# A decoder layer of gMLP, sparse attention and MLP on one core: two early tiles in a place of their own, a state copy cut into eight, norm sums moved, the last tile in halves

## The chip, the core and the metric

The kernel runs on one core of one Trainium2 chip. The metric is the device time of one execution in microseconds (us); lower is better. The median of three runs is 2820.18 us (2817.41 to 2821.86).

## What is computed

One layer for 512 prompt rows and 8 sample rows (TOK = 520 columns in the kernel, kept transposed, features on partitions), all in float32:

```
h   = rmsnorm(x) ; z = h @ w_in              # kv pairs, queries, v and u of the gMLP, gates
A   = u * (tril(w_sgu) @ rmsnorm(v) + b_sgu) # per chunk of 128 rows and per channel group
B   = gates * (compressed, selected, window attention)  # 8 heads, T5 bias; samples use caches and state
mix = sigmoid(g_a) * (A @ w_proj_gmlp) + sigmoid(g_b) * (B @ w_proj_nsa)
x2  = x + mix @ w_out
y   = x2 + square(relu(rmsnorm(x2) @ w_up)) @ w_down
```

Also returned: the raw k and v rows, the last chunk of v, and for the 8 samples the window state (`win`), which is a plain copy of the input `state` (8 x 256 x 512 floats, 4.2 MB) with one row appended on the host.

## The kernel before, in words

Five engine programs are written out by hand and synchronised by semaphores; each engine runs its list in order, so what stands where in each list is the schedule. Every product is done in three passes on rounded parts: a weight tile `w` is split into `w_hi` (ScalarE, ACT) and `w_lo` = w - w_hi (VectorE, DVE), the moving operand into `a_hi` and `a_lo`, and TensorE (PE) adds hi*hi, lo*hi and hi*lo. SP loads the raw weights.

**Units.** The products ahead of the MLP are 68 units plus 16 and 16 (`unit`, line 508): one unit is 128 output rows, 16 row tiles of x in 4 chunks c = 0 to 3 of 24 matmuls. ACT and DVE run `beside(u, jobs)`: for each chunk they split one chunk of the next unit, and then do `jobs[c]`, so a job at index c comes behind the split of chunk c. PE does `hooks[c]` behind chunk c: small products for the attention. Order: 12 kv units, 8 query units, 16 units of v and u (pairs, one pair for each sample b: the sample's attention is hooked into it, `smp_pair`), 32 gate units (four for each head h, with the prompt's attention), 16 projection units, 16 output units that give x2.

**Places of the change.**
- The first kv units go to the two tiles `z[:, 0]` and `z[:, 1]`, are scaled there (`first_scale`, 1325), stored from there by an ACT queue (`store`, 1007) and copied by GpSimd (POOL, 1939). `z_free` (1329) makes DVE wait for store and copy before unit n+2 overwrites the tile. Behind it in DVE's list stand `rel_rows` and the splits; PE waits for `rel_done` (616).
- Sample pair 0: at index 1 DVE does `windows_turned` (1419), which PE's hook 2 (`smp_values(0)`, `smp_turn_keys(0)`) waits for.
- After the last sample pair PE does `norm_sum(N_NORM_V)` into PSUM banks 4 and 5 (`aux[:, 0:2]`), waits until DVE's `mean` has read it, and starts the scores of head 0.
- POOL issues the copy `win <- state` as one DMA (2015) when v is normed, in head 0. The gate tiles' stores `merge_d <- z` (2023) are issued behind it, and DVE waits for them (`g_stored`, 1648).
- Between the gate units and the projections, the 16 mixed tiles are split to `a_hi`, `a_lo` (`mixed_chunk`): tiles 0 to 3 in the last gate unit, 4 to 15 behind it. The loads `g_in` (2034) wait for the last gate store.
- The MLP runs in NG = 16 groups. A group has 2 x 7 block products (`product`; r = 0, 1 and b = 0 to 6, block i = 7r + b; a Strassen-like scheme with weight sums `w_sums`) and 16 down tiles (`down_part`). Weights stay in 4 raw slots; `HI_RING` names the place of each block's `w_hi`. Eight-fold operand tiles `at_t` are made from x2; the last (index 7, from x2 tiles 14 and 15) can only be made when the last output unit is done: `first_pair` (1812). The sum of squares of x2 is gathered by POOL (`x2_spill`), summed over partitions by `norm_sum(N_NORM_X2)` in `up_first` (897), and turned into 1/rms by `x2_base`, `x2_guess`, `x2_scale`.
- At the end, for each of 16 output tiles: `y_in` adds the last down sum, `y_out` multiplies by r squared and adds x2, SP stores (502).

Of the kernel before, what the change touches and what calls it, by code (L numbers as in the profile page):

```python
# [42 lines left out]
EPS = 1e-6  # L43
# [35 lines left out]
HI_RING = (0, 1, 2) * 6 + (1, 0, 1, 2)  # L79
# [53 lines left out]
def build(nc, t):  # L133
    with ExitStack() as ctx:
# [75 lines left out]
        x_two = at("x_two", [P, KT, TOK], zone)  # L210
        u_t = at("u_t", [P, GRP, TOK], r1)
# [112 lines left out]
        norm_base = sem("norm_base")  # L324
        norm_guess = sem("norm_guess")
# [43 lines left out]

        aux3_made, aux3_read = sem("aux3_made"), sem("aux3_read")  # L370
# [12 lines left out]
        ff_used, ff_out = sem("ff_used"), sem("ff_out")  # L383
# [75 lines left out]
        def _(sp_):  # L459
# [47 lines left out]
        def _(pe):  # L507
# [34 lines left out]
            def norm_sum(n, src=None, made=None):  # L542
# [5 lines left out]
                for h in range(2):  # L548
                    last = pe.matmul(aux[:, h, 0:HT], ones[:, :], src[:, h * HT:(h + 1) * HT],  # L549
# [219 lines left out]
            with pe.Fori(1, DEC) as b:  # L769
# [119 lines left out]
            def up_first():  # L889
# [13 lines left out]
            def down_part(g, u, kts):  # L903
                o = DOWN_BANKS[u % 4]
                i = 2 * NP + u // 2
                for kt in kts:
# [3 lines left out]
                    for w, a, part in ((wh, fb_hi, 0), (wh, fb_lo, 1), (wl, fb_hi, 2)):  # L910
                        for h in range(2):
# [1252 lines left out]
```

## Time and profile before

| what | value |
|---|---|
| median of 3 runs | 2820.18 us |
| the profiled execution | 2819.64 us, its span 2818.0 us |
| mean granted TensorE clock | 0.994 |
| PE busy | 2792.2 us (99%) |
| weight loads | 2747.7 us (98%) |
| DVE, ACT, POOL busy | 56%, 34%, 8% |
| DMA engines, mean over the span | 110 GB/s |
| chain that ended last | PE 95%, DVE 2%, DMA 1%, ACT 1%, issue 1% |

Busy time is a share of the span; PE's is matmuls as the profile models them, so it can be busy and not at full rate. The clock is 1.00 at 2.4 GHz and 0.50 at 1.2 GHz; a stretch's value is the mean over it.

### The profile page before, as it was taken

The page shows a single profiled execution, that of the slowest core. Times are in us where ns is not written, and L with a number is a line of the kernel's source. Part 1 is how long each engine was busy: PE and PEld are TensorE (multiplying, and loading weights), DVE is VectorE, ACT ScalarE, POOL GpSimd, SP SyncE. Part 2 cuts the span into 40 slices and gives each one's busy share as a digit, 9 for nine tenths or more (in the row PEclk, how much of TensorE's full clock was granted, in tenths as well). Part 3 has the DMA queues.
Part 4 walks back from the last instruction along what each step waited for, and adds up shares of the span by engine and source line. Part 5 has one row for each costly group of instructions (what it writes and reads, how often), then busy time and mean ns, then how long its engine had stood idle before and what let it go on. Part 6 is the DMA issues. An engine that isn't in the chain of part 4 may idle for free.

```text
span 2818.0 us, 57713 instructions
## 1 busy us (share of the span) xinstructions
PE 2792.2 (99%) x22723; PEld 2747.7 (98%) x22723; DVE 1576.8 (56%) x2759; ACT 958.9 (34%) x1481; POOL 224.0 (8%) x337
## 2 busy tenths in 40 slices
PE   8999999999999999999999999999999999999999
PEld 8999899999999999999999999999999999999999
DVE  5433554454444454445576566665566655666658
ACT  5435433333333342223243223332233322333322
POOL 2100122210000010013310000000000000000000
PEclk9999999999999999999999999999999999999999
DMA  6533233342222224444432323322232223332225
GB/s 199 187 101 106 75 112 97 108 147 96 87 93 95 90 87 149 135 127 136 140 103 87 101 90 104 104 90 88 89 116 97 95 79 106 102 104 97 89 97 184
DMA packets 89235, 309.27 MB, mean 110 GB/s; under 512 B 11586, under 2 KB 11714, under 8 KB 89104
## 3 DMA queue, kind: packets, MB, share of 16 engines
q1 hardware_dynamic: 70112, 247.63, 27.0%
q0 software_dynamic: 16032, 55.42, 6.0%
q10 hardware_dynamic: 3024, 5.32, 0.6%
q8 instruction: 45, 0.74, 0.1%
q14 instruction: 22, 0.18, 0.0%
HBM read 287.23 MB, written 27.37 MB: 112 GB/s over the span
## 4 chain that ended last, share of the span: by engine, by line
PE 95%; DVE 2%; DMA 1%; ACT 1%; issue 1%; POOL 0%; SPq 0%; DVEq 0%; ACTq 0%; POOLq 0%
PE mm L535 39%; PE mm L912 13%; PE aux L912 13%; PE mm L857 12%; PE aux L857 9%; PE aux L640 1%; PE mm L609 1%; PE aux L794 1%; DMA merge_d<-z 1%; PE aux L783 1%; PE aux L784 1%; PE aux L807 1%; PE aux L805 1%; PE aux L549 0%; PE aux L756 0%
## 5 line engine op out<-in xcount | busy, mean ns | idle before, releaser
L1259 DVE TENSOR_TENSOR w_lo<-w_raw,w_hi 128x512 fp32r<-128x512 f32 x392 | 280.2, 716 | 632.7 <-ACT w_hi L954 631.5
L1738 DVE TENSOR_TENSOR w_lo<-w_raw,w_hi 128x1024 fp32r<-128x1024 f32 x288 | 352.8, 1225 | 390.1 <-ACT w_hi L1184 149.3
L535 PE MATMUL mm<-a_hi,w_hi 128*128 128x260 f32 x2624 | 549.0, 291 | 3.2 <-DVE rel_s L1293 2.0
L535 PE MATMUL mm<-a_hi,w_lo 128*128 128x260 f32 x2624 | 531.9, 284 | 0.0
L535 PE MATMUL mm<-a_lo,w_hi 128*128 128x260 f32 x2624 | 531.4, 284 | 0.0
L1184 ACT ACTIVATE w_hi<-w_raw 128x1024 fp32r<-128x1024 f32 x288 | 297.6, 1056 | 656.9 <-PE mm L912 432.6
L954 ACT ACTIVATE w_hi<-w_raw 128x512 fp32r<-128x512 f32 x392 | 246.3, 629 | 691.7 <-PE mm L535 668.5
L535 PEld LDWEIGHTS mm<-a_hi,w_hi 128*128 128x128 f32 x2624 | 408.4, 190 | 10.0 <-DVE w_lo L1259 3.5
L535 PEld LDWEIGHTS mm<-a_lo,w_hi 128*128 128x128 f32 x2624 | 408.6, 190 | 0.0
L535 PEld LDWEIGHTS mm<-a_hi,w_lo 128*128 128x128 f32 x2624 | 408.1, 190 | 0.0
L857 PE MATMUL mm<-at_t,w_hi 128*128 128x260 f32 x2048 | 372.8, 284 | 4.2 <-DVE at_t L1830 3.3
L857 PEld LDWEIGHTS mm<-at_t,w_hi 128*128 128x128 f32 x2048 | 316.4, 189 | 6.7 <-issue 3.5
L857 PE MATMUL mm<-at_t,w_lo 128*128 128x260 f32 x1024 | 289.5, 283 | 0.0
L857 PE MATMUL aux<-at_t,w_hi 128*128 128x260 f32 x1536 | 278.3, 283 | 1.0 <-DVE w_lo L1738 1.0
L857 PEld LDWEIGHTS aux<-at_t,w_hi 128*128 128x128 f32 x1536 | 236.7, 188 | 1.6 <-DVE w_lo L1738 1.6
L857 PE MATMUL aux<-at_t,w_lo 128*128 128x260 f32 x768 | 217.0, 283 | 0.0
L912 PE MATMUL aux<-fb_lo,w_hi 128*128 128x260 f32 x1024 | 207.6, 284 | 0.0
L912 PE MATMUL mm<-fb_lo,w_hi 128*128 128x260 f32 x1024 | 207.4, 284 | 0.0
L912 PE MATMUL mm<-fb_hi,w_lo 128*128 128x260 f32 x1024 | 206.2, 283 | 0.0
L912 PE MATMUL aux<-fb_hi,w_lo 128*128 128x260 f32 x1024 | 205.8, 282 | 0.0
L912 PE MATMUL mm<-fb_hi,w_hi 128*128 128x260 f32 x1024 | 205.4, 282 | 0.0
L912 PE MATMUL aux<-fb_hi,w_hi 128*128 128x260 f32 x1024 | 205.3, 282 | 0.0
(312 smaller groups left out, 4164.4 us busy)
## 6 DMA issues: line engine op xcount, KB each, us to landing
w_raw<-in_w_ff SPq DMA_DIRECT2D x256, 512.0 KB, 3.6
w_raw<-in_w SPq DMA_DIRECT2D x200, 512.0 KB, 3.7
merge_d<-z POOLq DMA_DIRECT2D x32, 260.0 KB, 2.4
g_in<-merge_d POOLq DMA_DIRECT2D x16, 520.0 KB, 4.8
x_back<-x_d POOLq DMA_DIRECT2D x8, 520.0 KB, 9.1
out_y_t<-y_acc SPq DMA_DIRECT2D x16, 260.0 KB, 2.0
pages<-in_cache_cmp POOLq DMA_DIRECT2D x16, 256.0 KB, 3.4
w_cmp<-in_w_cmp POOLq DMA_DIRECT2D x8, 512.0 KB, 4.6
```

The costliest lines, as they stand in the source:

```text
L535: last = pe.matmul(mm[:, 2 * v + h, 0:HT], w, a[:, kt, h * HT:(h + 1) * HT], start=first and k == 0 and part == 0, stop=final and k == CK ...
L609: last = pe.matmul(mm[:, 2 * u + h, 0:HT], w, a[:, kt, h * HT:(h + 1) * HT], start=kt == 0 and part == 0, stop=kt == KT - 1 and part == 2)
L640: last = pe.matmul(aux[:, 2 + kv, 0:NKV * (W_ALL + 1)], w_cmp[:, n % 2, jj, :], kv_t[:, NKV * kv:NKV * (kv + 1), j % STRIDE, j // STRIDE:j ...
L783: pe.matmul(aux[:, 0, 0:P * (i + 1)], qi, k_t[:, g, 0:P * (i + 1)], start=True, stop=True)
L784: pe.matmul(aux[:, 1, 0:P * (i + 1)], qi, k_t[:, 2 + g, 0:P * (i + 1)], start=True, stop=True)
L794: pe.transpose(aux[:, n, k * P:(k + 1) * P], src[:, k * P:(k + 1) * P], ident[:, :])
L857: last = pe.matmul(bank(BANKS[r][b]), w, at_t[:, j, e:e + HT], start=FRESH[b] and j == 0 and part == 0, stop=j == KP - 1 and part == 2, sk ...
L912: last = pe.matmul(bank(o + h), w, a[:, kt, h * HT:(h + 1) * HT], start=kt == 0 and part == 0, stop=kt == 3 and part == 2)
L954: run(w_hi[:, c, :], raw(u, c), ACT.Copy).then_inc(hi_split, 1)
L1184: run(ring_hi(i), fold(source(i)), ACT.Copy).then_inc(ff_hi, 1)
L1259: dve.tensor_tensor(w_lo[:, c, :], raw(u, c), w_hi[:, c, :].bitcast(F32), ALU.subtract).then_inc(lo_split, 1)
L1738: dve.tensor_tensor(ring_lo(i), fold(source(i)), ring_hi(i).bitcast(F32), ALU.subtract).then_inc(ff_lo, 1)
```

## The change

Eight edits at once:

1. `z_first` = two tiles of `x_two` hold units 0 and 1; `z_free` waits only from unit 4 on.
2. Sample pair 0: the hook and the jobs of index 2 go to index 3.
3. The sum for v's norm goes to banks 6 and 7 and ahead of the last sample's `attend`; waits for the banks move into `scores`.
4. The state copy leaves head 0; it becomes 8 DMAs, one for each sample, sample b when group b of the MLP has ended.
5. Mixed tiles 4 to 7 are split at index 3 of the last gate unit instead of behind it.
6. The start of the MLP: ACT makes one of the two scaled operands, `HI_RING` swaps places 1 and 2 so that block 1 does not wait for a weight sum, the operands come in three portions, and PE does block 1's product over index 6 late.
7. x2's norm: the last square by ACT in a tile of its own, the sum over partitions ahead of block 3, the guess and its Newton step spread over group 0 (tiles 12 to 15 of `y_acc`).
8. Last tile: `y_acc` is scaled and added early, the last down sums come half by half, two 133 KB stores, the second from ACT's queue. For this the last group stands outside PE's loop.

```diff
-HI_RING = (0, 1, 2) * 6 + (1, 0, 1, 2)
+HI_RING = (0, 2, 1) * 6 + (2, 0, 2, 1)
...
+        z_first = x_two[:, 2 * CH:2 * CH + 2, :]
...
+            sp_.wait_ge(y_done, MB)
+            sp_.dma_start(t["y_t"][MB - 1][:, 0:HT], y_acc[:, MB - 1, 0:HT]).then_inc(y_stored, 16)
...
-            smp_pair(0, [lambda: norm_sum(n_norm_q(NH - 1)), turn_windows,
+            smp_pair(0, [lambda: norm_sum(n_norm_q(NH - 1)), turn_windows, None,
                          lambda: (smp_values(0)(), smp_turn_keys(0)())])
-            pe.wait_ge(smp_read, DEC)
-            norm_sum(N_NORM_V, acc_v, (v_acc, GRP))
-            pe.wait_ge(norm_base, N_NORM_V + 1)
+            smp_pair(DEC - 1, [smp_values(DEC - 1), None, smp_turn_keys(DEC - 1)],
+                     lambda: norm_sum(N_NORM_V, acc_v, (v_acc, GRP), 2))
...
+                    pe.wait_ge(smp_read, DEC)
                     pe.matmul(aux[:, 1, 0:P * (i + 1)], qi, k_t[:, 2 + g, 0:P * (i + 1)], start=True, stop=True)
+                    pe.wait_ge(norm_base, N_NORM_V + 1)
...
+                    if b in (2, 3) and r == 0 and type(g) is int and g == 0:
+                        pe.wait_ge(at_ready, KP + b - 1)
+                    if b == 3 and r == 0 and type(g) is int and g == 0:
+                        norm_sum(N_NORM_X2, y_acc[:, MB - 4, :], (x2_added, 1))
...
-                product(0, 1, range(KP - 1))
-                norm_sum(N_NORM_X2, acc_x, (x2_squared, MB))
+                product(0, 1, range(KP - 2))
                 pe.wait_ge(at_ready, KP)
                 product(0, 0, [KP - 1])
-                product(0, 1, [KP - 1])
+                product(0, 1, [KP - 2, KP - 1])
...
+                    if final and u == MB - 1:
+                        for h in range(2):
+                            down_part(g, u, range(4), (h,))
...
-            ff_hi_in(0, 2, (at_ready, KP - 1))
-            ff_hi_in(0, 1, (chunk_done, CH * UNITS))
+            ff_hi_in(0, 1, (at_ready, KP - 1))
+            act.wait_ge(mm_read, U_OUT + 2 * MB - 1)
+            act.wait_ge(chunk_done, CH * UNITS)
+            run(ops_15[:, 0:2, :], halves(x2_14[:, :]), ACT.Copy, scale=g_mlp[:, 2 * KP - 2:2 * KP - 1]
+                ).then_inc(at_src, 1)
...
+            ff_hi_in(0, 2, (chunk_done, CH * UNITS))
+            act.wait_ge(mm_read, U_OUT + 2 * MB)
+            run(y_acc[:, MB - 3, :], x2_15[:, :], ACT.Square).then_inc(last_squared, 1)
...
-                    if first and n == 5:
-                        x2_guess()
+                    if first and n in (6, 8):
+                        x2_guess((n - 6) // 2)
...
-                if 2 <= n < U_Q + 2:
+                if 4 <= n < U_Q + 2:
                     dve.wait_ge(z_stored[n % 2], 16 * min(n // 2, U_Q // 2))
-                if 2 <= n < U_KV + 2:
+                if 4 <= n < U_KV + 2:
                     dve.wait_ge(z_copied, n - 1)
...
-            head(NH - 1, [[None] * CH] * 3 + [[lambda: mixed_chunk(0), None, None, None]])
+            head(NH - 1, [[None] * CH] * 3 + [[lambda: mixed(0, CK), None, None, lambda: (dve.wait_ge(u_mixed, NH), mixed(CK, GRP))]])
...
+            for h in range(2):
+                cols = slice(h * HT, (h + 1) * HT)
...
+                steps.did(dve.tensor_tensor(x_back[:, 0, cols], bank(DOWN_BANKS[(MB - 1) % 4] + h),
+                                            x_back[:, MB, cols], ALU.mult))
+                dve.tensor_tensor(y_acc[:, MB - 1, cols], y_acc[:, MB - 1, cols], x_back[:, 0, cols], ALU.add
+                                  ).then_inc(y_done, 1)
...
-            pool.dma_start(t["win"], t["state"]).then_inc(win_stored, 16)
...
+            for b in range(DEC):
+                pool.wait_ge(ff_used, BLOCKS * (b + 1))
+                pool.dma_start(t["win"][b], t["state"][b]).then_inc(win_stored, 16)
+            pool.wait_ge(win_stored, 16 * DEC)
```

DVE's list at the start of the MLP (`ops_120` is `ops_15`, `x_15_116` is x2 tile 15, `w_hi_127` the extra place `w_hi2`), before:

```order
L1720 TENSOR_TENSOR x_15_116<-mm,x_15_116 128x520
L1694 TENSOR_SCALAR ops_120<-x_15_116,gains 128x520
L1738 TENSOR_TENSOR w_lo<-w_raw,w_hi 128x1024
L1694 TENSOR_SCALAR ops_120<-x_14_115,gains 128x520
L1823 TENSOR_TENSOR at_t<-ops_120,at_t 128x2x260
L1700 TENSOR_TENSOR ops_120<-ops_120 128x520
L1702 TENSOR_TENSOR ops_120<-ops_120 128x260
L1704 TENSOR_TENSOR ops_120<-ops_120 128x260
L1738 TENSOR_TENSOR w_lo<-w_sum,w_hi_127 128x1024
L1828 TENSOR_TENSOR at_t<-ops_120,at_t 128x260
L1830 TENSOR_TENSOR at_t<-ops_120,at_t 128x1040
```

and with the change:

```order
L1751 TENSOR_TENSOR x_15_116<-mm,x_15_116 128x520
L1722 TENSOR_SCALAR ops_120<-x_15_116,gains 128x520
L1769 TENSOR_TENSOR w_lo<-w_raw,w_hi_127 128x1024
L1729 TENSOR_TENSOR ops_120<-ops_120 128x520
L1732 TENSOR_TENSOR ops_120<-ops_120 128x260
L1868 TENSOR_TENSOR at_t<-ops_120,at_t 128x2x260
L1734 TENSOR_TENSOR ops_120<-ops_120 128x260
L1872 TENSOR_TENSOR at_t<-ops_120,at_t 128x260
L1769 TENSOR_TENSOR w_lo<-w_sum,w_hi 128x1024
L1876 TENSOR_TENSOR at_t<-ops_120,at_t 128x260
L1878 TENSOR_TENSOR at_t<-ops_120,at_t 128x780
L1854 TENSOR_TENSOR y_acc<-acc_x,y_acc 128x520
```

One scaling is gone from DVE, part 4 of `at_t` (T2) comes ahead of the split of block 2, and a sum for the norm stands at the end.

DVE's list in the last gate unit, before:

```order
L1259 TENSOR_TENSOR w_lo<-w_raw,w_hi 128x512
L1285 TENSOR_TENSOR z<-mm,rstd 128x520
L1651 COPY q_t<-aux 128x128
L1631 TENSOR_TENSOR a_lo<-u_t,a_hi 128x520 x4
L1631 TENSOR_TENSOR a_lo<-q_t,a_hi 128x520 x8
```

and with the change:

```order
L1287 TENSOR_TENSOR w_lo<-w_raw,w_hi 128x512
L1660 TENSOR_TENSOR a_lo<-u_t,a_hi 128x520 x4
L1314 TENSOR_TENSOR z<-mm,rstd 128x520
L1680 COPY q_t<-aux 128x128
L1660 TENSOR_TENSOR a_lo<-q_t,a_hi 128x520 x8
```

Four splits now stand ahead of the last gate tile `z` and of the last `q_t`.

## Rows read from the trace of the kernel before

**Rows 1.** The page: busy time of the engines.

```profile
PE 2792.2 (99%) x22723; PEld 2747.7 (98%) x22723; DVE 1576.8 (56%) x2759; ACT 958.9 (34%) x1481; POOL 224.0 (8%) x337
```

**Rows 2.** PE's waits: us in total, times, longest.

```profile
PE mm L857 <- DVE at_t L1830: 3.3, 1, 3.3
PE aux L697 <- issue: 3.0, 1, 3.0
PE mm L535 <- DVE rel_s L1293: 2.0, 1, 2.0
PE aux L794 <- DVE p_c L1604: 1.9, 1, 1.9
PE mm L535 <- DVE a_lo L1631: 1.2, 1, 1.2
PE aux L783 <- DVE na L1274: 1.2, 1, 1.2
PE aux L857 <- DVE w_lo L1738: 1.0, 3, 0.4
```

**Rows 3.** Stretches: length, busy PE, PEld, DVE, ACT, POOL, clock, DMA share, GB/s.

```profile
320.80:324.80 4.00, 3.49 (x18) 3.52 (x19) 3.90 (x8) 0.69 (x1) 0.00 (x0) 0.57 0.39 135
401.00:408.00 7.00, 7.00 (x48) 7.00 (x48) 4.21 (x26) 2.55 (x3) 3.49 (x4) 0.76 0.48 150
556.00:564.00 8.00, 6.56 (x28) 5.73 (x29) 1.67 (x11) 2.99 (x8) 1.30 (x3) 0.57 0.57 197
617.00:623.00 6.00, 5.03 (x29) 4.97 (x30) 4.20 (x9) 0.80 (x2) 0.00 (x0) 0.72 0.29 89
1429.00:1435.00 6.00, 4.30 (x24) 4.33 (x25) 4.19 (x5) 2.15 (x3) 0.00 (x0) 0.72 0.14 27
1861.60:1871.40 9.80, 9.80 (x83) 9.66 (x82) 7.84 (x8) 3.85 (x6) 0.00 (x0) 1.00 0.00 0
```

**Rows 4.** Timeline near 57 us: start, us, engine, line, out<-in [idle before].

```profile
57.68 0.70 DVE L1285 TENSOR_TENSOR z<-mm,rstd 128x520 f32<-128x520 f32 x1 [3.42 <-issue]
```

**Rows 5.** Timeline of sample pair 0, DVE.

```profile
320.80 0.40 DVE L1421 COPY vc_p<-aux 31x256 f32<-31x256 f32 x1
322.58 0.76 DVE L1359 SCALAR_TENSOR_TENSOR q_t<-z,gains,nr 128x520 f32<-128x520 f32 x1
```

**Rows 6.** Timeline in head 0: gate store and the tile waiting for it.

```profile
593.69 0.65 POOL L2023 DMA_DIRECT2D merge_d<-z  x1 [0.72 <-POOL z L2022]
610.80 0.70 DVE L1285 TENSOR_TENSOR z<-mm,rstd 128x520 f32<-128x520 f32 x1 [4.54 <-DMA merge_d<-z]
```

**Rows 7.** Timeline behind the last gate unit.

```profile
1053.40 4.96 DVE L1631 TENSOR_TENSOR a_lo<-q_t,a_hi 128x520 fp32r<-128x520 f32 x8
1055.11 1.46 POOL L2034 DMA_DIRECT2D g_in<-merge_d  x2 [2.76 <-DMA merge_d<-z]
1059.49 0.69 DVE L1677 TENSOR_TENSOR na<-mm,g_in 128x520 f32<-128x520 f32 x1
```

**Rows 8.** Timeline at the start of the MLP, DVE.

```profile
1429.37 1.23 DVE L1830 TENSOR_TENSOR at_t<-ops,at_t 128x1040 fp32r<-128x1040 f32 x1
```

**Rows 9.** A steady MLP group: first loads, and ACT behind them.

```profile
1871.45 21.88 SPq L480 DMA_DIRECT2D w_raw<-in_w_ff  x7
...
1878.00 2.13 ACT L1184 ACTIVATE w_hi<-w_raw 128x1024 fp32r<-128x1024 f32 x2 [3.33 <-DMA w_raw<-in_w_ff]
```

**Rows 10.** DMA issues of the page: KB each, us to landing.

```profile
w_raw<-in_w_ff SPq DMA_DIRECT2D x256, 512.0 KB, 3.6
out_y_t<-y_acc SPq DMA_DIRECT2D x16, 260.0 KB, 2.0
```

**Rows 11.** Timeline of the end, DVE.

```profile
2813.39 0.70 DVE L1786 TENSOR_TENSOR y_acc<-aux,y_acc 128x520 f32<-128x520 f32 x1 [0.71 <-PE aux L912]
2814.86 0.70 DVE L1796 TENSOR_TENSOR y_acc<-y_acc,x_back 128x520 f32<-128x520 f32 x1
```

**Rows 12.** The state copy's line: us to landing.

```profile
DMA to landing us min/median/max: 17.8/17.8/17.8
```

More of the change, by code:

```diff
@@ L548, in norm_sum @@
                 for h in range(2):
-                    last = pe.matmul(aux[:, h, 0:HT], ones[:, :], src[:, h * HT:(h + 1) * HT],
+                    last = pe.matmul(aux[:, banks + h, 0:HT], ones[:, :], src[:, h * HT:(h + 1) * HT],
                                      start=True, stop=True)
@@ L910, in down_part @@
                     for w, a, part in ((wh, fb_hi, 0), (wh, fb_lo, 1), (wl, fb_hi, 2)):
-                        for h in range(2):
+                        for h in hs:
                             last = pe.matmul(bank(o + h), w, a[:, kt, h * HT:(h + 1) * HT],
@@ L935, in _ @@
             down_group(0)
-            with pe.Fori(1, NG) as g:
+            with pe.Fori(1, NG - 1) as g:
                 up_pair(g, 0)
@@ L1125, in mixed, with mixed_tiles @@
                 run(a_hi[:, kt, :], src, ACT.Copy).then_inc(act_hi, 1)
-            def mixed_chunk(c):
-                for kt in range(CK * c, CK * (c + 1)):
+            def mixed_tiles(first, end):
+                for kt in range(first, end):
                     mixed(kt)
@@ L1153, in _ @@
             act.wait_ge(aux3_read, 6 * NH)
-            for c in range(1, CH):
-                mixed_chunk(c)
+            mixed_tiles(GRP, KT)
             def split_hi(count, dst, src, func=ACT.Copy):
@@ L1214, in hidden_hi, with x2_guess @@
                 run(fb_hi[:, n, :], c_out[n // 2][n % 2][:, :], ACT.Copy).then_inc(ff_bhi, 1)
-            def x2_guess():
-                act.wait_ge(norm_base, N_NORM_X2 + 1)
-                steps.did(run(y_acc[:, 1, :], y_acc[:, 0, :], ACT.Ln))
-                steps.did(run(y_acc[:, 1, :], y_acc[:, 1, :], ACT.Exp, scale=-0.5))
-                run(y_acc[:, 2, :], y_acc[:, 1, :], ACT.Square).then_inc(norm_guess, 1)
+            def x2_guess(n):
+                base, r, q, r2 = (y_acc[:, MB - 4 + k, :] for k in range(4))
+                if n == 0:
+                    act.wait_ge(norm_base, N_NORM_X2 + 1)
+                    steps.did(run(r, base, ACT.Ln))
+                else:
+                    steps.did(run(r, r, ACT.Exp, scale=-0.5))
+                    run(q, r, ACT.Square).then_inc(norm_guess, 1)
             def ff_group(g, ahead):
@@ L1268, in beside, with mean @@
                         jobs[c]()
-            def mean(n, count, w=None):
+            def mean(n, count, w=None, banks=0):
                 dve.wait_ge(summed, n + 1)
-                dst, src = (halves(na[:, :]), aux[:, 0:2, 0:HT]) if w is None else (na[:, 0:w], aux[:, 0, 0:w])
+                dst, src = ((halves(na[:, :]), aux[:, banks:banks + 2, 0:HT]) if w is None else
+                            (na[:, 0:w], aux[:, 0, 0:w]))
                 dve.tensor_scalar(dst, src, 1.0 / count, EPS, ALU.mult, ALU.add).then_inc(norm_base, 1)
@@ L1625, in probs_out, with mixed @@
                 dve.tensor_copy(pt_cmp[0:32, :], aux[0:32, 2, 0:P]).then_inc(pt_made, 1)
-            def mixed_chunk(c):
-                for kt in range(CK * c, CK * (c + 1)):
+            def mixed(first, end):
+                for kt in range(first, end):
                     src = u_t[:, kt, :] if kt < GRP else q_t[:, kt - GRP, :]
@@ L1662, in _ @@
                 head(h)
-            head(NH - 1, [[None] * CH] * 3 + [[lambda: mixed_chunk(0), None, None, None]])
+            head(NH - 1, [[None] * CH] * 3 + [[lambda: mixed(0, CK), None, None, lambda: (dve.wait_ge(u_mixed, NH), mixed(CK, GRP))]])
             dve.wait_ge(aux3_read, 6 * NH)
-            for c in range(1, CH):
-                mixed_chunk(c)
+            mixed(GRP, KT)
             with dve.Fori(0, MB // 2) as i:
@@ L1850, in ff_pair @@
                 w_sums(g, r, 3)
+                if first:
+                    dve.wait_ge(x2_added, 1)
                 c_in(g, r, 0)
@@ L1878, in ff_group @@
                 hidden_lo(g, 3)
+                if first:
+                    x2_scale(2)
                 for k in range(MB // 2):
@@ L2050, in x2_spill @@
                     x_in(i + 1, p)
+                if type(m) is int and m == MB - 1:
+                    return
                 if not (type(m) is int and m == 0):
```

155 lines of the change are left out of this document (96 added, 59 removed).

## The prediction

> **What bounds the kernel now.** The engine totals come first [rows 1]: PE is busy 2792 of 2818 us and its weight loads 2748, every other engine under 60%. The change removes no matmul, so only two things are to be had: the 26 us in which PE stands still, and what PE loses while its clock is low. The list of PE's waits says where it stands still [rows 2]: nearly every row is a single event at a seam between two stages, none is a wait that recurs in a loop. The stretches give the clock [rows 3]. A matmul stream of 24 takes 2.88 us at 1.00 (2.4 GHz) and twice that at 0.50 (1.2 GHz). In 401 to 408 PE is busy for all 7.00 us and the clock is 0.76, so 7 x 0.24 = 1.7 us are lost; this fall follows the sample's `attend`, ten matmuls of 4 columns that take 2.2 us, and it recurs in five of the eight sample pairs. Four other stretches of rows 3 are low: right behind the wait of sample pair 0, at the end of the sample loop (twice as much), behind the state copy's wait, and behind the wait at the MLP's start. The mean clock of 0.994 leaves 0.006 x 2818 = 17 us, which is ten such losses: five in the loop, five at the seams. So a wait's price here is its length and the slow matmuls behind it.
>
> **Edit 1, the first tiles.** DVE idles 3.42 us at 57.68 before it scales unit 2 [rows 4], because the tile is still being stored and copied; `rel_rows` stands behind it, and PE waits 2.0 us for that [rows 2]. With its own tiles the scaling can start when the work before it ends, at 54.3; everything behind comes 3.4 us sooner and PE's 2.0 us go. Next in line would be the split of unit 4, 1.5 us ahead of need. Gain 2.0, at worst 0.
>
> **Edit 2, sample pair 0.** PE waits 3.0 us [rows 2] for DVE's `vc_p`, which lands at 321.2 [rows 5]. With the hook one chunk later PE spends 2.9 of these on chunk 3 and waits 0.3. But then only one chunk (2.9) lies between the key transposes and the scores that need the keys. DVE ends `q_t` at 323.3 [rows 5], then has two splits (1.2), the value copy (0.4), the keys (0.7) and four small copies (0.5): 326.2. PE is there at 321.3 + 1.1 + 2.9 = 325.3 and waits 0.9. Of the wait 3.0 - 0.3 - 0.9 = 1.8 is won. The clock of 0.57 behind it [rows 3] costs 4.0 x 0.43 = 1.7, which I expect to go. Gain 3.5; 1.8 if the clock falls anyway, 4.7 if the new waits don't come.
>
> **Edit 3, v's norm.** PE waits 0.3 for the last sample's result and 1.2 for `mean` [rows 2]. With the sum ahead of `attend` only DVE's copy (0.2) and `mean` (0.7) follow the last matmul, and 0.4 of scores run beside them: a wait of about 0.5, so 0.9 is won. Stretch 556 to 564 is at 0.57 [rows 3]: 8.0 x 0.43 = 3.4, less what falls on idle time, about 2.6. The `attend` stays, so one fall may stay: I take half, 1.3. Gain 2.2, from 0.9 to 3.5.
>
> **Edit 4, the state copy.** Now 4.2 MB are copied by one DMA, which takes 17.8 us [rows 12]; the gate store issued behind it at 593.69 lands only when DVE has waited 4.54 us [rows 6], then softmax and `p_c` are late and PE waits 1.9 [rows 2] and runs at 0.72 for 6 us (1.7) [rows 3]. Without it a 260 KB store takes some 2 to 5 us [rows 10], 8 us before DVE wants it. Gain 3.6; 1.9 if that clock fall has another cause. The cost comes in the MLP. Copy b starts when PE ends group b, and in a steady group the DMA engines are idle for the first 9.8 us: share 0.00 from 1861.6 [rows 3], first load at 1871.45 [rows 9]. One copy is an eighth of the bytes: 17.8 / 8 = 2.2 us at least, and no more than the 3.6 of a 512 KB load with as much again for the writing, 7 us [rows 12, 10]. Both ends fit into 9.8, so I take 0. POOL has nothing else to do there, and nothing waits for it before `x_back` in the last group. A rule speaks against the edit: the Trainium skill, "DMA: Bandwidth & Descriptors", section "Rules for kernel authors", wants at least 1 MiB per DMA for full bandwidth; by the fit of that page (2.0 us and 436 GB/s) eight copies take 25.6 us of transfer against 11.6 for one. I go by the idle stretch of the trace, in which no engine waits for such a transfer.
>
> **Edit 5, the mixed tiles.** PE waits 1.2 us for tile 4's `a_lo` [rows 2]. With tiles 4 to 7 split early, chunk 1 runs on. But ACT and DVE do these four (2.5 us) ahead of the last gate tile and the last `q_t`, so both come 2.6 us later. Tiles 8 to 11 are split at 1056.0 against PE's need at 1055.2, wait 0.8, so 0.4 would be left. The gate store moves too, and the load of `g_in` behind it: issued at 1055.11, it landed by 1059.49 [rows 7]; 2.6 later is 1062.1, and with DVE's 0.7 the first bank pair is free at 1062.8. PE wants it at 1061.8 for the next unit and today starts that unit at 1062.3. So this seam ends 0.5 later than now: -0.5, from -1.5 to +1.2.
>
> **Edit 6, the MLP's start.** PE waits 0.45 for `w_lo` of block 1 (same list up to there, stays) and 3.3 for `at_t` [rows 2], whose last piece DVE starts at 1429.37 [rows 8]; then 6 us run at 0.72 (1.7) [rows 3]. Following the new list with today's durations: operand sums end at 1424.1, the first portion at 1425.1, the T2 portion at 1425.9, `w_lo` of block 2 at 1427.2, the last portion at 1428.5, the added sum of squares at 1429.1. PE has its work without these until 1426.3, waits 0.9 for block 2 and, at 1430.2, 0.2 for block 3. Of 3.75 us 2.2 are won, with the clock 3.9; from 2.2 to 5.0.
>
> **Edit 7, x2's norm.** Its DVE and ACT work in the first block pairs makes PE wait three times, 1.2 us in sum (the row with 1.0 is most of it [rows 2]). Spread out, one piece on ACT (2.6 us with a table load) stands ahead of the split of block 11, which has 0.6 us to spare in DVE and PE: about 0.6 is lost. Gain 0.6, from -1.0 to 1.2.
>
> **Edit 8, the end.** PE ends at 2813.35; three DVE operations of 0.70 follow and the last ends at 2815.56 [rows 11], then 2.4 us to the end of the span. With halves the tail is four of 0.45; but DVE is about 1 us behind PE in the last tiles, and the two early operations on tile 15 (1.4 us) push it to 2813.5 before it can start them. It ends near 2815.3. With the smaller store I take 0.5, from 0 to 1.5.
>
> **Sum.** 2.0 + 3.5 + 2.2 + 3.6 - 0.5 + 3.9 + 0.6 + 0.5 = 15.8 us. The profiled execution took 2819.64, 0.5 below the median: 2803.8 by its own time, 2804 for the median. All bad ends together give a gain of 4.3 (2816), all good ends 22.7 (2797).
>
> **Rival A, the clock falls in the sample loop change in number.** No wait goes ahead of them, and pairs 0 and 1 have none while the next five have one each, with the same code: their number is not fixed by the program. Edits 1 and 2 move the loop by 5 us. All five may go: 5 x 1.7 = 8.5 less, 2795.5. Against it: the three runs of before differ by 4.4 us only, so it happened in none of them. The Trainium skill, "TensorE: Matmul & The Clock Gate", section "What's actually happening", says that the activity window runs freely and does not restart with a kernel; by that rule the number may differ from run to run. Chance 0.16.
>
> **Rival B, the waits come back elsewhere.** Pair 0's keys, block 2's `w_lo`, block 11 and `g_in` are each within 1 us of being late by the sums above, and each renewed wait may bring its clock fall back (1.7). With half of the gain gone: 2811, between 2809 and 2814. Chance 0.18.
>
> **Rival C, slower.** The copies meet the weight loads. ACT already waits 3.3 us for a load in each group [rows 9], and DVE behind it has no slack worth the name. If a copy took more than 9.8 us, or were issued late, the load would be late by 2.5 us or so and PE with it, plus a clock fall: 8 x 4.2 = 34, 2838. The point is a copy of 9.8 us, over four times the lower bound. Chance 0.04.
>
> **Rival D, eight transfers cost more than one.** If loads wait behind them, what counts is their sum: 8 x 3.6 = 29 us at a 512 KB load's time [rows 10] against 17.8 [rows 12]. The 11 us more take most of the gain: 2815. For it: they share the DMA engines with the loads; against it: the idle 9.8 us. Chance 0.04. The Trainium skill's rule of 1 MiB, "DMA: Bandwidth & Descriptors", is this case, with 14 us by its fit.
>
> **The numbers.** The forecast has 0.58. A measurement here tells about 0.2% (5.6 us) from no change. Faster: 0.58 + 0.16 + 0.18 = 0.92; same 0.04; slower 0.04. The range 2796 to 2812 takes in the forecast's own bounds, half of A and two thirds of B.
>
> **What the next profile would show.** Right: no wait for `rel_s`; under 1.5 us of waits in pair 0; clock 1.00 near 320, 615 and 1430; DVE without a DMA wait in head 0; steady groups still 86.5 us long with 8 copies that land within 7 us. Wrong: groups 1 to 8 longer than the later ones (C), waits of 1 us or more at the new places (B), a sample loop whose clock differs by more than one fall (A).

## The result and the profile after

| kernel | median us | range | ratio to before, 95% interval |
|---|---|---|---|
| before (5 executions) | 2819.86 | 2817.41 to 2821.86 | |
| changed (5 executions) | 2805.87 | 2804.78 to 2809.45 | 0.9953 (0.9938 to 0.9967) |

The change makes the kernel 14.0 us faster; 15.8 were forecast. The profiled execution of the changed kernel took 2809.45 us (span 2808.0), the slowest of the five, and its span is only 10.0 us shorter than in the profile before. The sections below bear on both gaps.

The page of the changed kernel, busy time of the engines, as [rows 1]:

```profile
PE 2790.3 (99%) x22723; PEld 2745.9 (98%) x22723; DVE 1578.6 (56%) x2763; ACT 960.5 (34%) x1484; POOL 224.3 (8%) x341
```

PE's waits in it, as [rows 2] (us in total, times, longest):

```profile
PE mm L540 <- DVE rel_s L1322: 1.6, 1, 1.6
PE mm L863 <- DVE w_lo L1769: 1.1, 2, 0.7
PE aux L863 <- DVE w_lo L1769: 1.1, 3, 0.4
PE mm L540 <- DVE a_lo L1660: 0.8, 1, 0.8
PE mm L540 <- DVE na L1705: 0.7, 1, 0.7
PE aux L725 <- issue: 0.6, 1, 0.6
PE aux L791 <- DVE na L1303: 0.2, 1, 0.2
PE aux L746 <- DVE sp L1543: 0.2, 1, 0.2
```

The 3.3 us for `at_t`, the 3.0 of sample pair 0 and the 1.9 for `p_c` are gone; the 1.6 for `rel_s` was to go and did not. The stretches that answer to [rows 3], in the same order:

```profile
326.00:330.00 4.00, 3.62 (x26) 2.45 (x27) 2.78 (x12) 2.44 (x3) 2.90 (x3) 1.00 0.70 239
399.00:406.00 7.00, 7.00 (x49) 7.00 (x49) 4.22 (x25) 2.55 (x4) 3.40 (x4) 0.76 0.49 145
555.00:563.00 8.00, 7.78 (x49) 7.42 (x50) 2.78 (x14) 4.02 (x9) 2.41 (x4) 0.79 0.57 193
609.40:615.40 6.00, 6.00 (x53) 5.99 (x53) 3.54 (x8) 1.50 (x3) 0.00 (x0) 1.00 0.30 90
1416.00:1422.00 6.00, 5.18 (x40) 4.97 (x41) 5.38 (x10) 4.88 (x8) 0.00 (x0) 1.00 0.10 37
1850.60:1860.40 9.80, 9.80 (x82) 9.68 (x82) 7.99 (x9) 4.01 (x6) 0.49 (x1) 1.00 0.18 54
```

Three of the four low stretches at a seam between two stages are at 1.00, and the double fall at 556 is a single one. The fall inside the sample loop (second row) stayed. The last row is the idle stretch of a group, with a state copy in it. All eight copies land fast (the view of their line):

```profile
L2142 POOL DMA_DIRECT2D out_win<-in_state x8: 486/486/525, 1503.7 to 2110.6; - x8
...
DMA to landing us min/median/max: 3.5/3.7/3.9
```

**Where the time went.** The same operations were looked up in both profiles, and the change of their difference from place to place was taken:

| stretch | forecast | gained |
|---|---|---|
| start, same code (x arrives) | 0 | -0.7 |
| edit 1, up to unit 4 | 2.0 | 0.4 |
| edit 2, up to pair 0's scores | 3.5 | 3.7 |
| edit 3 and the sample loop | 2.2 | 0.5 (2.2 less one more clock fall, 1.7) |
| edit 4, head 0 | 3.6 | 3.7 |
| edit 5, up to the second projection pair | -0.5 | -0.7 |
| edits 6 and 7, up to the end of group 0's hidden tiles | 4.5 | 5.0 |
| groups 1 to 15 | 0 | -2.4 |
| edit 8, from PE's end to the end of the span | 0.5 | 0.6 |
| sum | 15.8 | 10.1 |

(The spans themselves differ by 10.0; the rest is rounding.) Three rows are off: edit 1, the loop and the groups; the start is 0.7 later with the same code. A clock fall is read by 1 us stretches; each one costs 1.70 or 1.71 us. Before there are ten (17.1 us), in the changed kernel seven (11.9 us), and all seven follow an `attend`: those of pairs 1 to 7.

### The profile page after: what moved, and what is told of

Read it like the earlier page. It is cut to its first block, busy times and chain, and to the rows that moved or that the text cites. A ratio compares the mean times of both kernels' runs of the same rounds, so it can differ in the third digit from the quotient of the medians.

```text
span 2808.0 us, 57688 instructions
## 1 busy us (share of the span) xinstructions
PE 2790.3 (99%) x22723; PEld 2745.9 (98%) x22723; DVE 1578.6 (56%) x2763; ACT 960.5 (34%) x1484; POOL 224.3 (8%) x341
## 4 chain that ended last, share of the span: by engine, by line
PE 75%; issue 18%; DVE 3%; POOL 2%; ACT 1%; DMA 1%; POOLq 0%; SPq 0%; ACTq 0%; DVEq 0%
PE mm L540 25%; PE aux L919 13%; PE mm L919 13%; PE mm L863 12%; PE aux L863 9%; PE mm L614 1%; PE aux L645 1%; POOL z L2090 1%; DVE w_lo L1769 1%; ACT w_hi L1197 0%; PE aux L761 0%; POOL merge_d L2091 0%; DVE w_lo L1287 0%; PE aux L554 0%; PE aux L659 0%
```

## The experiments

Every one is the changed kernel with the edit shown, unless it says otherwise.

| label | median us | range | ratio to before, 95% |
|---|---|---|---|
| e1_copies_later | 2807.49 | 2804.60 to 2809.48 | 0.9956 (0.9943 to 0.9970) |
| e2_attend_split | 2798.98 | 2795.95 to 2799.15 | 0.9925 (0.9912 to 0.9939) |
| e3_copy_in_head | 2808.45 | 2806.99 to 2809.77 | 0.9960 (0.9946 to 0.9973) |
| e4_mixed_behind | 2806.80 | 2804.23 to 2808.92 | 0.9954 (0.9940 to 0.9967) |
| e5_end_as_before | 2806.00 | 2804.57 to 2808.84 | 0.9954 (0.9937 to 0.9971) |
| e6_start_as_before | 2812.78 | 2809.26 to 2816.62 | 0.9976 (0.9966 to 0.9985) |
| e7_places_swapped | 2817.72 | one execution | |
| e8_copies_with_loads | 2805.80 | 2804.55 to 2810.24 | 0.9959 (0.9944 to 0.9974) |
| e9_together | 2795.12 | 2792.29 to 2797.73 | 0.9910 (0.9897 to 0.9924) |
| e10_v_norm_back | 2800.98 | 2798.24 to 2802.17 | 0.9929 (0.9914 to 0.9944) |
| e11_copies_in_burst | 2813.70 | one execution | |
| e12_hook_back | 2797.84 | 2797.55 to 2800.61 | 0.9920 (0.9905 to 0.9936) |

**1. Why edit 1 gained little: GpSimd holds VectorE up.** In the changed kernel DVE scales unit 2 without a wait, at 54.91 in place of 57.68 [rows 4]. But its two splits behind that take until 61.04 (timeline of the changed kernel: start, us, engine, line, out<-in), and the second of them is most of it:

```profile
54.91 0.69 DVE L1314 TENSOR_TENSOR z<-mm,rstd 128x520 f32<-128x520 f32 x1
56.14 4.98 DVE L1287 TENSOR_TENSOR w_lo<-w_raw,w_hi 128x512 fp32r<-128x512 f32 x2 [0.54 <-ACT w_hi L968]
61.04 0.67 DVE L1319 COPY rel_row<-aux 8x512 f32<-8x512 f32 x1
```

POOL in the same time, its last DMA issue and three copies:

```profile
56.29 1.16 POOL L2004 DMA_DIRECT2D kv_t<-in_pos  x1 [4.77 <-issue]
57.44 2.11 POOL L2008 COPY kv_t<-x_two 128x512 f32<-128x512 f32 x2
59.48 1.08 POOL L2008 COPY kv_t<-z 128x512 f32<-128x512 f32 x1
```

The same place in the kernel before:

```profile
56.50 3.15 POOL L1939 COPY kv_t<-z 128x512 f32<-128x512 f32 x3
58.30 2.51 DVE L1259 TENSOR_TENSOR w_lo<-w_raw,w_hi 128x512 fp32r<-128x512 f32 x2
```

Edit 1 did not move the copies. Counted from the start of `mean` (47.45 before, 48.19 in the changed kernel), the first starts at 9.05 before and at 9.25 now, both times when POOL's last `kv_t<-in_pos` issue ends. Before, VectorE stood still for its tile while the first two ran, and only the third met its splits. With edit 1 the second split is at hand when the first copy starts, and it ends behind the third. Whether the copies hold it up is the question of the next run, in which they come later.

```diff
             for n in range(U_KV):
-                pool.wait_ge(z_made, n + 1)
+                pool.wait_ge(z_made, max(n + 1, 4))
```

> The changed kernel with one edit: GpSimd's copies of units 0 to 2 into kv_t wait until unit 3 is scaled. Theory H (VectorE is held up by GpSimd's copies): in the changed kernel VectorE's second split at 56.7 lasts until 61.04 while GpSimd copies from 57.44 to 60.56, where such a split takes 0.69 alone. With the copies moved behind 64 the split ends at about 58.7, rel_s at about 59.6, and the wait of 1.6 us ahead of unit 4 is gone; the copies then meet splits that have 2.1 us of idle time ahead of each. Time: 1.6 us less than the changed kernel, about 2804.3. Theory I (the split is late for another reason, ScalarE's w_hi or the DMA of the first tiles): the split stays at about 4.3 us, rel_s at 62.0, no gain. If the loop's clock falls change in number, each is 1.7 us more or less, and is read from the clock.

DVE in e1_copies_later:

```profile
52.82 0.69 DVE L1314 TENSOR_TENSOR z<-mm,rstd 128x520 f32<-128x520 f32 x1
54.05 1.30 DVE L1287 TENSOR_TENSOR w_lo<-w_raw,w_hi 128x512 fp32r<-128x512 f32 x2 [0.54 <-ACT w_hi L968]
55.26 0.67 DVE L1319 COPY rel_row<-aux 8x512 f32<-8x512 f32 x1
```

Both splits take 1.30 us, `rel_s` comes 10.1 us after the start of `mean` in place of 13.8, PE's wait for it is gone, and unit 4 comes 1.8 us earlier relative to `mean`. So theory H holds in the profile. The Trainium skill, "SBUF — State Buffer", section "Terms", says the two engines share a pair of ports that one of them holds for a whole instruction while the other is blocked. The trace agrees in that the split did not get on while copies ran (0.69 us became 4.2 to 4.4 us beside three copies in eight profiles); why it lost to all three in a row, though its record starts 0.5 to 0.7 us ahead of the first, no run shows. I had these copies in view for the tile's reuse and not for what they do to DVE. The median did not fall (2807.49, where 2804.3 was expected); executions of one kernel differ by up to 7.4 us (e6_start_as_before), and two profiles show a reason in this very place: in e2_attend_split and e5_end_as_before, with the copies where the changed kernel has them, the splits and the copies took turns (both splits 3.07 us together in e2_attend_split, the copies longer than alone) and PE had no wait for `rel_s`. In the other eight that keep the copies there, the changed kernel's among them, it had 1.4 to 1.6 us. Unmoved, the copies win or lose 1.8 us by a matter of timing.

**2. The clock falls in the sample loop.** They follow `attend`, ten matmuls of 4 columns in a row. PE in the changed kernel:

```profile
397.92 0.41 PE L540 MATMUL mm<-a_hi,w_lo 128*128 128x260 f32 x2
398.17 0.95 PE L761 MATMUL aux<-pt_s,stage 128*128 128x4 f32 x8
398.98 0.36 PE L762 MATMUL aux<-pt_s,vx_s 65*128 65x4 f32 x2
399.20 1.03 PE L761 MATMUL aux<-pt_s,stage 128*128 128x4 f32 x8
400.10 0.36 PE L762 MATMUL aux<-pt_s,vx_s 65*128 65x4 f32 x2
400.32 0.67 PE L540 MATMUL mm<-a_hi,w_hi 128*128 128x260 f32 x2
```

(The profile splits each into two records.) The pair of 260 columns behind them takes 0.67 in place of 0.40: the clock has fallen to 0.50.

```diff
                         for w, a, part in ((wh, ah, 0), (wh, al, 1), (wl, ah, 2)):
                             ...
+                        if middle and c == CH - 1 and k == CK // 2 - 1:
+                            middle()
...
-                     [smp_scores(b), None, smp_turn_probs(b), lambda: (last() if last else None, smp_attend(b)())])
+                     [smp_scores(b), None, smp_turn_probs(b), lambda: (last() if last else None, smp_attend(b, (1,))())],
+                     middle=smp_attend(b, (0,)))
```

> The changed kernel with one edit: the ten 4-column matmuls of a sample's attend are issued in two halves with 12 matmuls of the unit between them, in place of ten in a row. In the changed kernel the clock falls for 3.4 us after seven of the eight attends, 1.7 us lost each, 11.9 in all, with PE busy throughout. Theory F (it is the row of narrow matmuls, 2.2 us, that brings the clock down): with halves of 1.1 us the falls go, all or most of them: 7 x 1.7 = 11.9 us less, about 2794. Theory G (a fall depends on the whole pair's narrow work, or on something else in the pair, and not on the row): the falls stay, 2806, and the profile shows 6 or 7 falls again. Each fall that goes is worth 1.7 us, so the number in the profile and the time must agree.

PE in e2_attend_split, then the stretch behind:

```profile
393.04 0.95 PE L763 MATMUL aux<-pt_s,stage 128*128 128x4 f32 x8
393.84 0.36 PE L764 MATMUL aux<-pt_s,vx_s 65*128 65x4 f32 x2
394.07 0.49 PE L540 MATMUL mm<-a_hi,w_hi 128*128 128x260 f32 x2
...
395.59 0.95 PE L763 MATMUL aux<-pt_s,stage 128*128 128x4 f32 x8
396.40 0.36 PE L764 MATMUL aux<-pt_s,vx_s 65*128 65x4 f32 x2
```

```profile
396.00:403.00 7.00, 7.00 (x60) 7.00 (x61) 4.43 (x27) 3.10 (x5) 3.77 (x4) 1.00 0.51 150
```

No fall is left in the whole profile (mean clock 1.0). The loop is 10.7 us shorter than in the changed kernel, 1.2 less than the seven falls. The median is 6.9 us lower, and not the 11.9 of the expectation. Theory F holds in this profile: the same ten matmuls, in two rows of five, leave the clock alone. Its other four executions are 1.7 to 3.2 us longer at a mean clock of 0.999, so one or two falls are likely left in them; they have no trace. This was rival A of the prediction, but as something that one can act on.

**3. Edit 4, the state copy.**

```diff
+            pool.dma_start(t["win"], t["state"]).then_inc(win_stored, 16)
...
-            for b in range(DEC):
-                pool.wait_ge(ff_used, BLOCKS * (b + 1))
-                pool.dma_start(t["win"][b], t["state"][b]).then_inc(win_stored, 16)
-            pool.wait_ge(win_stored, 16 * DEC)
+            pool.wait_ge(win_stored, 16)
```

> The changed kernel with edit 4 undone: the state copy is one DMA in head 0 again. My theory: VectorE waits 4.5 us for the gate tile's store, PE 1.9, and the clock falls once: 3.6 us more than the changed kernel, 2809.5. Nothing is won back in the MLP, groups 1 to 8 keep their length. Rival (the copies in the MLP cost something, the 1.2 us by which group 1 is longer in the changed kernel): group 1 gets 1.2 us shorter, and the kernel is only 2.4 us slower. Rival (the clock fall at 619 has another cause than the wait): only the 1.9 us come back.

DVE waits for the gate store again, 4.0 us, and PE 1.3 for `p_c`:

```profile
605.00 0.70 DVE L1314 TENSOR_TENSOR z<-mm,rstd 128x520 f32<-128x520 f32 x1 [3.96 <-DMA merge_d<-z]
```

The stretch around it, with the clock in the third column from the end:

```profile
605.00:620.00 15.00, 13.68 (x118) 13.46 (x117) 10.23 (x34) 6.65 (x15) 2.14 (x5) 1.00 0.33 106
```

Head 0 costs 1.6 us more than in the changed kernel and not 3.6: the clock stays at 1.00 here. It does so in e7_places_swapped (section 7) too, which has the kernel before's code in head 0, a wait of 3.87 us in DVE and one of 1.2 in PE:

```profile
615.00:625.00 10.00, 8.79 (x77) 8.58 (x75) 7.49 (x22) 3.89 (x7) 0.48 (x2) 1.00 0.32 100
```

So the fall at 618 in the kernel before is no fixed price of that wait. The median is 2.6 us higher. Group 1 takes 87.59 us here too, without a copy in it (87.64 in the changed kernel): its extra length is not the copies'.

**4. Edit 5, the mixed tiles.** Tiles 4 to 7 again behind the last gate unit:

```diff
-            head(NH - 1, [[None] * CH] * 3 + [[lambda: mixed(0, CK), None, None, lambda: (dve.wait_ge(u_mixed, NH), mixed(CK, GRP))]])
+            head(NH - 1, [[None] * CH] * 3 + [[lambda: mixed(0, CK), None, None, None]])
...
-            mixed(GRP, KT)
+            mixed(CK, KT)
```

> The changed kernel with edit 5 undone: mixed tiles 4 to 7 are split behind the last gate unit again. My theory: PE waits 1.2 us for tile 4 in place of 0.8 for tile 8 and 0.7 for g_in, so the kernel is 0.5 us faster than the changed one (the profile of after shows this seam 0.7 us longer than before). Rival: edit 5 pays once the other edits are there, 0.3 to 1.2 us slower without it. A difference this small lies within a measurement's scatter, so the seam is read from the profile: the start of the last bank pair of the projections relative to the last softmax.

PE waits once, 1.2 us, in place of 0.8 and 0.7, and the seam is 0.7 us shorter in the profile (0.5 forecast). The median (2806.80) can't tell it.

**5. Edit 8, the end.** Its parts in SP, PE, ACT and DVE undone; in PE:

```diff
-            with pe.Fori(1, NG - 1) as g:
+            with pe.Fori(1, NG) as g:
...
-            up_pair(NG - 1, 0)
-            up_pair(NG - 1, 1)
-            down_group(NG - 1, True)
```

> The changed kernel with edit 8 undone: the last group is inside PE's loop again, and the last tile is added, scaled and stored whole. Seen in the traces so far: the last group takes 86.38 us before, and 86.55 to 87.89 in the changed kernel and its variants; there PE fetches five more packets of instructions through the DMA engines in the last two groups, and one wait for w_lo of 0.3 us follows a weight load that came late. Theory J (the last group outside the loop costs instruction fetches that meet the weight loads): the last group takes 86.4 to 86.6 again and the wait at its block 12 is gone, the tail is 0.4 us longer: 0.2 to 0.8 us less in sum than the changed kernel. Rival (edit 8 is worth its 0.4 us, and the length of the last group scatters by itself): the last group still takes 86.6 to 87.9, and the kernel is 0.4 us slower.

Lengths of groups, from last hidden tile to last hidden tile:

| kernel | 1 | typical of 2 to 14 | 15 | sum of 1 to 15 |
|---|---|---|---|---|
| before | 86.46 | 86.53 | 86.38 | 1298.40 |
| changed | 87.64 | 86.60 | 87.22 | 1300.78 |
| e5_end_as_before | 86.94 | 86.60 | 86.42 | 1299.27 |
| e6_start_as_before | 86.44 | 86.53 and 86.61 in turn | 86.81 | 1299.24 |
| e7_places_swapped | 86.50 | 86.60 | 86.42 | 1299.82 |
| e11_copies_in_burst | 88.57 | 87.2 to 87.8 (3 to 8) | 87.03 | 1306.82 |

The last group is back at 86.42; with edit 8 it took 86.56 to 87.89 in the ten profiles that have it, 86.9 in the mean. The tail from PE's end to DVE's last operation is 0.38 longer, to the end of the span 0.56. So edit 8 wins 0.6 and gives back 0.1 to 1.5, 0.5 in the mean: it comes out about even, and the median (2806.00) shows no difference. Here is what differs in that group, the DMA queues of the changed kernel:

```profile
q1 hardware_dynamic: 2282, 8.30, 31.0%
q8 instruction: 2, 0.03, 0.2%
```

The queue of kind instruction is read here as PE's fetches of the program's code. In the kernel before and in e5_end_as_before, where PE runs the last group inside its loop, no instruction queue moves anything in that group. That such fetches meet the weight loads is a reading of these rows and of PE's 0.33 us wait for `w_lo` at 2746.03; no run isolates it.

**6. Edits 6 and 7, the MLP's start.** Their parts in PE, ACT, DVE and POOL undone, `HI_RING` too.

> The changed kernel with edits 6 and 7 undone, so that the MLP starts as before. My theory: from x2's last tile to the last hidden tile of group 0 the kernel before takes 5.0 us longer than the changed one, which was forecast as 3.9 + 0.6 = 4.5; that comes back, with a clock fall of 1.7 us behind the wait for at_t. Against it stands what the steady groups cost: they take 86.60 us in the changed kernel and all its variants, against 86.53 before, and group 1 takes 87.2 to 88.1 against 86.46. If that comes from edit 6 (places 1 and 2 of w_hi swapped), it goes too: 14 x 0.07 + 1.2 = 2.2 us back, and the kernel is only 2.8 us slower than the changed one, about 2808.7. If it does not come from edit 6, groups stay as they are, and it is 5.0 us slower, about 2810.9.

The wait for `at_t` is back, 3.3 us, with a fall twice as long as the one of [rows 3]:

```profile
1419.00:1425.00 6.00, 3.47 (x16) 3.50 (x17) 4.72 (x6) 2.98 (x4) 0.00 (x0) 0.63 0.06 6
```

The stretch up to group 0's hidden tiles takes 6.4 us more; with a single fall it would be 4.7. Group 1 is 1.2 us shorter, and the groups together 1.5. The median, 2812.78, lies above both cases of the expectation, 6.9 us above the changed kernel; the second half of the fall is 1.7 of it, the rest is not accounted for. Nor is the fall a fixed price of this wait: e7_places_swapped waits 3.3 us for `at_t` too, and has no fall behind it:

```profile
1426.00:1434.00 8.00, 5.22 (x44) 5.25 (x44) 6.81 (x8) 4.57 (x7) 0.00 (x0) 1.00 0.23 67
```

**7. Places swapped alone, on the kernel before.**

```diff
-HI_RING = (0, 1, 2) * 6 + (1, 0, 1, 2)
+HI_RING = (0, 2, 1) * 6 + (2, 0, 2, 1)
...
-            ff_hi_in(0, 2, (at_ready, KP - 1))
-            ff_hi_in(0, 1, (chunk_done, CH * UNITS))
+            ff_hi_in(0, 1, (at_ready, KP - 1))
+            ff_hi_in(0, 2, (chunk_done, CH * UNITS))
```

> The kernel before with one part of edit 6 alone: the places 1 and 2 of w_hi are swapped for all blocks, the order of the work is kept. If the swapped places make the steady groups longer, they take 86.60 us each here and group 1 about 87.6; if not, 86.53 and 86.46 as in the kernel before. The rest of the kernel stays as before, about 2820, within one clock fall of 1.7 us.

The steady groups take 86.60, and the work in them is the same in the same order (only ACT's first two `w_hi` of group 0 change their order): 0.07 us each, 1.0 in all. Which place is slow and why stays open. Group 1 is 86.50: its extra 1.1 us comes from edits 6 and 7 but not from the places. In group 1 three weight loads are issued 54 to 55 us after the last hidden tile of group 0, and ACT waits for the last. In all eleven profiles with edits 6 and 7, two packets of the instruction queues fall between 53.6 and 59.2 us; in the kernel before, in this one and in e6_start_as_before none does, the nearest come at 51.5 and from 59.4 on. That fits, and is argued only.

**8. Are the copies free because the DMA engines idle?** Two runs issue them later.

```diff
-                pool.wait_ge(ff_used, BLOCKS * (b + 1))
+                pool.wait_ge(ff_used, BLOCKS * (b + 1) + 7)
```

> The changed kernel with each of the eight state copies issued seven blocks later, when three weight loads are issued within 1.4 us, in place of the stretch in which the DMA engines are idle. Theory (rival C of the prediction is real, and it is the idle stretch that makes the copies free): each copy lands later than the 3.7 us of now, 6 us or more, the loads beside it come 1.3 to 3.6 us later, ScalarE's w_hi with them, and PE waits 1 to 3 us in each of groups 1 to 8, perhaps with a clock fall of 1.7 us: 8 to 38 us slower than the changed kernel, my value 8 x 2 = 16, 2822. Rival (the loads have slack, or the queues share without loss): groups 2 to 8 still take 86.6 us, no change.

Groups and median (2805.80) are unchanged, where 2822 was expected, but the run tells little: the copy, issued at 1521.0, fell into another idle stretch and landed after 3.7 us. The second has `+ 3`:

> The changed kernel with each state copy issued three blocks later than in it. In e8_copies_with_loads (seven blocks later) the copy fell into another stretch in which the DMA engines were idle, so it met no load. Three blocks later it is issued at the same time as three weight loads that land 5 us later, and of which ScalarE waits for the last. If the copies are free only because they find the DMA engines idle: each adds its own 512 KB read and written to 1.5 MB of loads, the last load comes 1.3 to 3.6 us later, and groups 1 to 8 take 88 to 90 us in place of 86.6, groups 9 to 14 still 86.6. If the loads go ahead of it in their own queue, 86.6 throughout.

ACT in a steady group of e11_copies_in_burst, as the second of [rows 9]:

```profile
1868.86 2.01 ACT L1197 ACTIVATE w_hi<-w_raw 128x1024 fp32r<-128x1024 f32 x2 [4.36 <-DMA w_raw<-in_w_ff]
```

4.36 in place of 3.33: the loads come 1.0 us later, and groups 1 to 8 take 699.9 us in place of 693.8, 0.8 us each; groups 9 to 14 are mostly back at 86.6. There is no clock fall. So the mechanism of rival C exists and the idle stretch is what avoids it, but its price here is 6 us and not 34.

**9. Edits 2 and 3 without the loop's falls**, both on e2_attend_split.

```diff
-            smp_pair(DEC - 1, [smp_values(DEC - 1), None, smp_turn_keys(DEC - 1)],
-                     lambda: norm_sum(N_NORM_V, acc_v, (v_acc, GRP), 2))
+            smp_pair(DEC - 1, [smp_values(DEC - 1), None, smp_turn_keys(DEC - 1)])
+            pe.wait_ge(smp_read, DEC)
+            norm_sum(N_NORM_V, acc_v, (v_acc, GRP))
+            pe.wait_ge(norm_base, N_NORM_V + 1)
```

> e2_attend_split, in which the clock never falls, with edit 3 undone: the sum for v's norm goes to banks 4 and 5 behind the last attend, and PE waits for it ahead of head 0. This is edit 3's price in waits alone: 0.3 for the last sample's result and 1.2 for mean, against 0.2 left: 1.3 us slower than e2_attend_split, 2800.3, if the clock stays at 1.00. If 1.5 us of waiting are enough to bring the clock down after the narrow matmuls, 1.7 us more, 2802.0.

PE waits 1.1 and 1.2 us, and the clock falls for twice the usual time:

```profile
545.00:553.00 8.00, 5.99 (x26) 5.43 (x27) 2.28 (x13) 3.73 (x9) 1.50 (x4) 0.61 0.60 197
```

The seam is 4.5 us longer than in e2_attend_split, the median 2.0, where 1.3 or 3.0 were expected. In this profile the clock fell at these waits even with `attend` in halves, as it had at 556 in [rows 3]; one profile does not say how often it does.

> e2_attend_split with edit 2 undone: the hook of sample pair 0 stands behind chunk 2 again. PE waits 3.0 us for vc_p again in place of 0.6 + 0.2, and the clock may fall behind that wait (1.7 us), as it did at 321 in the kernel before. With the fall 3.9 us slower than e2_attend_split, 2802.9; without it 2.2 us slower, 2801.2.

(Its edit: the three lines of edit 2 in PE, ACT and DVE undone.) The profile has the wait of 3.0 us and one fall at 321, and this part is 3.5 us longer, as forecast. But the median is 2797.84, no higher than e2_attend_split's. Two of its four executions have a mean clock of 1.0, so no fall there; the rest of the contradiction is scatter elsewhere (start 2.2 us, `rel_s` 1.8), which neither set of four or five resolves. Edit 2's 3.5 is shown in profiles alone.

**10. Together.** The edits of e1, e2, e4 and e5.

> The changed kernel with everything that the runs so far spoke for: GpSimd's three copies later (e1_copies_later), attend in two halves (e2_attend_split), mixed tiles 4 to 7 behind the last gate unit (e4_mixed_behind), the end as before (e5_end_as_before). e2_attend_split alone had 2798.98. From there: up to 1.6 for the copies (its profile happened to have no wait for rel_s, so 0 in some executions), 0.7 for the mixed tiles, 0.2 to 1.0 for the last group, less 0.4 for the tail: 1 to 3 us less, 2797, between 2796 and 2798, with no clock fall in the profile. If the gains get in each other's way: 2799.

2795.12 us, 24.1 below the kernel before and 10.8 below the changed kernel. Its profile has no wait for `rel_s`, no clock fall and a last group of 86.41. That is 3.9 below e2_attend_split, where 1 to 3 were expected. It beats both kernels.

## Why the prediction was right, and where not

The median moved by 14.0 of the 15.8 us forecast, but in the two profiles compared only 10.0 to 10.1 are found. That the medians come so close is in part luck, and the terms say more than the sum.

- **Edit 1** is the step that failed: "everything behind comes 3.4 us sooner and PE's 2.0 us go". The scaling came 3.5 us sooner; `rel_s`, two splits behind it, came 0.4 sooner, since POOL's three copies held the second split up for 3.7 us. They stood where they had stood before; VectorE's wait for the tile had kept it out of their way. 0.4 for 2.0. The forecast asked what is late next in DVE's own list and not what runs on POOL at the new time.
- **Edit 2**: 3.7 for 3.5. The new wait for the keys is 0.6 where 0.9 was expected, the one of 0.3 at the hook did not come, and one of 0.2 for the first turned probabilities (`sp`) came that the forecast did not have.
- **Edit 3**: 2.2 for 2.2, and the guess of half a pair of falls was right for this profile: one of two stayed, the one behind the `attend`. Over the eight profiles with the same code it was a lucky choice of execution: one fall in three of them, none in four, and a double one in e3_copy_in_head.
- **Edit 4**: 3.7 for 3.6 in the profiles compared. e3_copy_in_head and e7_places_swapped show that 1.7 of it is a fall that comes in some executions only; without it the edit is worth 1.5 to 2.0. The cost in the MLP was 0 as taken; the copies landed in 3.7 us, within the 2.2 to 7 forecast.
- **Edit 5**: -0.7 for -0.5, with waits of 0.8 at tile 8 (0.8 worked out) and 0.7 at `g_in` (1.0 worked out).
- **Edits 6 and 7**: 5.0 for 4.5; the waits were 0.44 and 0.67 where 0.45 and 0.9 were expected, the clock stayed up. 1.7 of the gain is the fall behind `at_t`, which came once before, twice in e6_start_as_before and not at all in e7_places_swapped, with the same wait.
- **Groups 1 to 15** were taken at nothing and cost 2.4: 1.0 by the swapped places, 1.1 in group 1, 0.8 in the last, which stands outside the loop, less 0.6 by which the kernel before had one long group (87.16). A steady group waits 3.3 us for a load [rows 9]; that row was used for rival C and not for edits 6 and 8.
- **Edit 8**: 0.6 for 0.5, from PE's end to the end of the span; what it costs in the last group stands above.
- **The clock**: in the profiles compared the seam falls went as forecast, though those at 618 and 1430 can be absent without the change: e7_places_swapped, which has only the places of edit 6, has neither. Rival A was put low because the three runs of before differ by 4.4 us "so it happened in none of them"; but later executions of the kernel before have mean clocks from 0.992 (2824.40 us) to 0.995 (2815.74), which is more than three falls apart. In the loop there were six in place of five: rival A's mechanism, its number off by one and with the other sign. The Trainium skill's freely running window, cited there, agrees with what the executions show: eight profiles with the same code in the loop have seven (three of them) or six falls in it, pair 7's counted, one of them double.
- **The range**: 2796 to 2812 was said to take in the forecast's own bounds; its bad end, 2816, lies outside. The measured 2805.87 does not depend on it.
- **The median** gained 4.0 us more than the 10.0 between the spans of the two profiles. Only the profiled executions have a trace, so the account is argued. In profiles with the same start `mean` comes between 46.0 and 48.2 us (48.2 in the one of the changed kernel), `rel_s` costs 0 or 1.6, a fall 1.7: the profiled execution had the worse side of the first two, and its last group cost 0.8.

## What to carry over

Before work is moved to an earlier time, look at what the other engines do at that time: here GpSimd's copies, which nobody had moved, took back most of what VectorE's wait had given. A wait can hide such a meeting. A row of narrow matmuls that keeps PE "busy" can cost afterwards nearly as much as it takes itself (1.7 us behind 2.3); cutting it into two, with wide matmuls between, was worth as much as half of this whole change. A fall of the clock behind a wait is not a fixed part of the wait's price: the same wait had it in one execution and not in another. And a recurring group without slack has to be measured when anything around it changes, even code that only moves it out of a loop.

## What was not expected of the hardware

- The clock fell to 0.50 with PE busy for all 7.00 us of a stretch, each time behind ten matmuls of 4 columns; in the four profiles with rows of five no fall follows them in the loop. The Trainium skill, "TensorE: Matmul & The Clock Gate", section "What's actually happening", calls the low state idle; here no idle time stands ahead of it.
- A fall costs 1.70 or 1.71 us, or twice that, in all profiles, and its number differs between executions of the same code.
- VectorE's 0.69 us operation took about 4.3 us beside three GpSimd copies of 1.1 each, in eight of the ten profiles that keep edit 1 and the copies' place; in the other two the engines took turns and it was 1.6.
- Behind the same 3.3 us wait of PE for `at_t` the clock fell once, twice or not at all, in three profiles.
- A swap of two weight places in SBUF, with the same order of work in these groups, made each steady group 0.07 us longer.
